# Three token tiles of 88 rows, and a gate product of two columns, in a two-layer decoder trunk

## What is computed

```
logits = (h @ router).astype(jnp.float32)
top_v, top_i = lax.top_k(logits, TOP_K)
gates = jax.nn.softmax(top_v, axis=-1)
combine = jnp.sum(jax.nn.one_hot(top_i, N_EXPERTS) * gates[..., None], axis=-2)
for e in range(N_EXPERTS):
    y = y + combine[..., e:e + 1] * swiglu(h, wg[e], wu[e], wd[e])
```

## Time and profile before

| what | us |
|---|---|
| median of 3 runs | 1030.96 |
| the three runs | 1040.16, 1030.94, 1030.96 |
| span of the profiled execution, first to last instruction | 1036.4 |
| PE busy in it | 961.1 (93%) |
| DVE, ACT, POOL busy | 700.9, 583.8, 193.1 |
| mean granted clock of TensorE | 0.953 |

### The profile page before, as it was taken

One profiled execution on the slowest core, in us unless ns is written; L12 is line 12 of the kernel. 1 busy time (PEld: TensorE's weight loads), 2 busy tenths in 40 slices (PEclk: granted clock), 3 DMA queues, 4 the chain that ended last, 5 costly groups with the idle time before them and its releaser, 6 DMA issues.

```text
span 1036.4 us, 16514 instructions
## 1 busy us (share of the span) xinstructions
PE 961.1 (93%) x5967; PEld 859.6 (83%) x5967; DVE 700.9 (68%) x816; ACT 583.8 (56%) x727; POOL 193.1 (19%) x160
## 2 busy tenths in 40 slices
PE   1798999999999999899979999999999999999998
PEld 0698989999999999798957777787878787878787
DVE  0579747476656547974463356888888888888863
ACT  0565447554445346544442356777777877777742
POOL 0217308421212121730630000010101000000000
PEclk9999879999999999987975899999999999999997
DMA  9374204776699537420342247999898989898921
GB/s 276 86 202 121 82 1 143 199 219 182 182 250 260 159 105 201 122 82 1 113 163 84 86 138 316 389 345 343 330 358 327 364 307 382 301 385 293 376 83 43
DMA packets 171160, 217.62 MB, mean 210 GB/s; under 512 B 6896, under 2 KB 141232, under 8 KB 170974
## 3 DMA queue, kind: packets, MB, share of 16 engines
q1 hardware_dynamic: 163287, 206.25, 59.5%
q10 hardware_dynamic: 6455, 5.54, 1.8%
q0 software_dynamic: 1376, 5.27, 1.6%
HBM read 210.06 MB, written 7.43 MB: 210 GB/s over the span
## 4 chain that ended last, share of the span: by engine, by line
PE 66%; DVE 14%; ACT 8%; issue 6%; POOL 3%; DMA 2%; ACTq 2%; DVEq 0%; SPq 0%; POOLq 0%
PE bank L1599 21%; PE bank L1329 9%; PE bank L1331 8%; PE bank L1330 8%; DVE sb_w_lo L1103 6%; PE bank L1573 4%; ACT sb_w_hi L733 3%; PE bank L1358 2%; PE bank L1469 2%; PE bank L1399 2%; PE bank L1653 2%; ACTq L510 1%; DMA sb_raw<-in_ffn_w_up_dram 1%; DVE at_act_e L1206 1%; POOL at_state L467 1%
## 5 line engine op out<-in xcount | busy, mean ns | idle before, releaser
L890 DVE TENSOR_TENSOR sb_w_lo<-sb_raw,sb_w_hi 128x1024 fp32r<-128x1024 f32 (+1 forms) x116 | 161.8, 1397 | 79.8 <-ACT sb_w_hi L521 77.9
L1329 PE MATMUL bank<-at_act_hi,sb_w_hi 128*128 128x264 f32 x672 | 193.7, 288 | 9.5 <-DVE sb_w_lo L890 6.7
L521 ACT ACTIVATE sb_w_hi<-sb_raw 128x1024 fp32r<-128x1024 f32 (+1 forms) x116 | 126.9, 1101 | 133.9 <-PE bank L1331 114.5
L1103 DVE TENSOR_TENSOR sb_w_lo<-sb_raw,sb_w_hi 128x1408 fp32r<-128x1408 f32 (+1 forms) x104 | 154.4, 1497 | 58.2 <-ACT sb_w_hi L733 58.2
L1331 PE MATMUL bank<-at_act_hi,sb_w_lo 128*128 128x264 f32 x672 | 191.2, 285 | 0.0
L1330 PE MATMUL bank<-at_act_lo,sb_w_hi 128*128 128x264 f32 x672 | 191.1, 284 | 0.0
L1103 DVE TENSOR_TENSOR sb_w_lo<-at_raw_e,sb_w_hi 128x1408 fp32r<-128x1408 f32 (+1 forms) x112 | 158.8, 1450 | 28.3 <-ACT sb_w_hi L733 28.1
L733 ACT ACTIVATE sb_w_hi<-sb_raw 128x1408 fp32r<-128x1408 f32 (+1 forms) x104 | 131.3, 1262 | 73.0 <-PE bank L1599 72.8
L733 ACT ACTIVATE sb_w_hi<-at_raw_e 128x1408 fp32r<-128x1408 f32 (+1 forms) x112 | 138.4, 1243 | 42.2 <-PE bank L1599 38.5
L1329 PEld LDWEIGHTS bank<-at_act_hi,sb_w_hi 128*128 128x128 f32 x672 | 127.7, 190 | 10.2 <-issue 8.3
L1330 PEld LDWEIGHTS bank<-at_act_lo,sb_w_hi 128*128 128x128 f32 x672 | 127.7, 190 | 0.1
(11 more groups left out here) (263 smaller groups left out, 1631.8 us busy)
## 6 DMA issues: line engine op xcount, KB each, us to landing
sb_raw<-in_moe_w_up_dram SPq DMA_DIRECT2D x36, 704.0 KB, 7.2
at_raw_e<-in_moe_w_down_dram SPq DMA_DIRECT2D x49, 512.0 KB, 4.5
at_raw_e<-in_moe_w_gate_dram SPq DMA_DIRECT2D x35, 704.0 KB, 7.8
sb_raw<-in_w_in_dram SPq DMA_DIRECT2D x40, 512.0 KB, 4.0
sb_raw<-in_moe_w_gate_dram SPq DMA_DIRECT2D x29, 704.0 KB, 6.3
sb_raw<-in_moe_w_down_dram SPq DMA_DIRECT2D x39, 512.0 KB, 4.3
at_raw_e<-in_moe_w_up_dram SPq DMA_DIRECT2D x28, 704.0 KB, 6.3
sb_raw<-in_ffn_w_gate_dram SPq DMA_DIRECT2D x22, 512.0 KB, 3.9
```

The lines of the kernel that those rows point to most:

```text
L521: act.activation(w_hi[s][:, 0:kts, :], raw[s][:, 0:kts, :], ACT.Copy).then_inc(hi_done, 1)
L890: dve.tensor_tensor(w_lo[s][:, 0:kts, :], raw[s][:, 0:kts, :], w_hi[s][:, 0:kts, :].bitcast(f32), ALU.subtract).then_inc(lo_done, 1)
L1103: dve.tensor_tensor(lo, raw_e[raw_slot(j, turn)][:, 0:kts_cols, :], hi.bitcast(f32), ALU.subtract).then_inc(moe_lo, 1)
L1329: pe.matmul(out[:, 0:T], w_hi[s][:, k, :], hi[:, c, :], start=(c == 0), stop=False)
```

## The change

The three tiles become 88 rows each. The last one holds the prompt's last 80 tokens and the 8 sample tokens, so its load and its store are two DMAs each. Where DVE did two instructions for the wide tiles and the small one, it does one on 88 rows. For the gate of each slot DVE makes two parts of `gates`, one rounded to fp32r and the rest, next to each other (`gate_parts`), PE takes both as two columns of one product with fp32r operands, and DVE adds the two results with a reduction where it copied before. PE waits for step 24 (`HALVED`) there, where it waited for step 26.

```diff
--- before.py
+++ after.py
@@ -22,7 +22,9 @@
 EPS = 1e-6
 CAP = 128
 SEG = 128
-TOKEN_TILES = ((0, 128), (128, 128), (256, DEC))
+ROWS = T // 3
+TOKEN_TILES = ((0, ROWS), (ROWS, ROWS), (2 * ROWS, ROWS))
+LAST_PROMPT = SEQ - 2 * ROWS
 LEVELS = (1, 2, 4, 8, 16, 32, 64)
 PAD = 16
 
@@ -116,6 +118,7 @@
         rstd_tok = sb("rstd_tok", [128, 3])
         tops = sb("tops", [128, 4, 3])
         gates = sb("gates", [128, 3, N_EXPERTS])
+        gate_parts = sb("gate_parts", [128, 3, N_EXPERTS, 2], f32r)
         slot = sb("slot", [128, 3, N_EXPERTS])
         over = sb("over", [128, 3, N_EXPERTS])
         slot_gate = sb("slot_gate", [128, N_EXPERTS])
@@ -277,7 +280,7 @@
         HG_SUMS = ((5, slice(0, HEADS * SEG), slice(0, SEG)), (6, slice(0, HEADS * DEC), slice(SEQ, T)), (4, slice(0, HEADS * SEG), slice(SEG, SEQ)))
         PIECES = ((0, 512), (512, 512), (1024, 384))
 
-        CHOSEN, GAP, ROUTED = 9, 17, 26
+        CHOSEN, GAP, HALVED, ROUTED = 8, 16, 24, 27
 
         SQUARED = [0] + [KT + n * (2 * KT - 1) for n in range(4)]
         NORM_SUMS = ((3, 0), (4, 0), (4, 1))
@@ -377,12 +380,13 @@
                             sp.dma_start(dst[:, :, :], a[name][0][ds(e, 1), :, ds(f * 128, 128)].rearrange("a (k p) n -> p (a k) n", p=128)).then_inc(all_w, 16)
                         sp.dma_start(down_w_all[:, :], a["moe_w_down"][0][ds(e, 1), ds(f * 128, 128), :].rearrange("a p n -> p (a n)")).then_inc(all_w, 16)
             sp.end_ifs()
-            for i, (_, rows) in enumerate(TOKEN_TILES):
+            for i, (t0, rows) in enumerate(TOKEN_TILES):
                 sp.wait_ge(y_left, i + 1)
                 sp.wait_ge(y_right, i + 1)
-                dst = o["y_prompt"][0, 128 * i:128 * (i + 1), :] if i < 2 else o["y_sample"][:, 0, :]
-                sp.dma_start(dst, y_rows[0:rows, i, :]).then_inc(y_out, 16)
-            sp.wait_ge(y_out, 16 * 3)
+                prompt = min(rows, SEQ - t0)
+                sp.dma_start(o["y_prompt"][0, t0:t0 + prompt, :], y_rows[0:prompt, i, :]).then_inc(y_out, 16)
+            sp.dma_start(o["y_sample"][:, 0, :], y_rows[LAST_PROMPT:ROWS, 2, :]).then_inc(y_out, 16)
+            sp.wait_ge(y_out, 16 * 4)
 
 
         @block.gpsimd
@@ -500,9 +504,10 @@
         @block.scalar
         def _(act):
             for i in range(2):
-                act.dma_start(x_rows[:, i, :], a["x_prompt"][0, 128 * i:128 * (i + 1), :]).then_inc(x_in, 16)
-            act.dma_start(x_rows[0:DEC, 2, :], a["x_sample"][:, 0, :]).then_inc(x_in, 16)
-            act.wait_ge(x_in, 48)
+                act.dma_start(x_rows[0:ROWS, i, :], a["x_prompt"][0, ROWS * i:ROWS * (i + 1), :]).then_inc(x_in, 16)
+            act.dma_start(x_rows[0:LAST_PROMPT, 2, :], a["x_prompt"][0, 2 * ROWS:SEQ, :]).then_inc(x_in, 16)
+            act.dma_start(x_rows[LAST_PROMPT:ROWS, 2, :], a["x_sample"][:, 0, :]).then_inc(x_in, 16)
+            act.wait_ge(x_in, 64)
             act.dma_start(consts[:, C_BEFORE:], a["consts"][:, C_BEFORE:]).then_inc(tables_in, 16)
             act.dma_start(pool_past[:, :], a["state_pool"][0].rearrange("b r c -> (b r) c")).then_inc(past_in, 16)
             act.dma_start(pool_w[:, :, :], a["pool_w"][0].rearrange("g c d -> c g d")).then_inc(pool_w_in, 16)
@@ -744,7 +749,7 @@
             act.dma_start(h_saved, scaled_m[:, :, :].rearrange("p k t -> p (k t)")).then_inc(h_out, 16)
             split_e(1, FE)
 
-            act.wait_ge(rstd_turned, 2)
+            act.wait_ge(rstd_turned, 1)
             for i, (_, rows) in enumerate(TOKEN_TILES):
                 for c in range(2):
                     act.wait_ge(h_turned, 2 * i + c + 1)
@@ -1122,10 +1127,8 @@
             dve.tensor_tensor(logit_rows[:, :], bank[6][0:N_EXPERTS, 0:T], rstd[0:N_EXPERTS, :], ALU.mult).then_inc(logits_scaled, 1)
             dve.wait_ge(logits_zeroed, 1)
             dve.wait_ge(tokens_turned, 1)
-            n_last = TOKEN_TILES[2][1]
-            spread_rstd = bank[5][:, 128:512].rearrange("p (i t) -> p i t", i=3)
-            dve.tensor_copy(rstd_tok[:, 0:2], spread_rstd[:, 0:2, 0]).then_inc(rstd_turned, 1)
-            dve.tensor_copy(rstd_tok[0:n_last, 2:3], spread_rstd[0:n_last, 2, 0:1]).then_inc(rstd_turned, 1)
+            spread_rstd = bank[5][0:ROWS, 128:512].rearrange("p (i t) -> p i t", i=3)
+            dve.tensor_copy(rstd_tok[0:ROWS, :], spread_rstd[:, :, 0]).then_inc(rstd_turned, 1)
             steps = [0]
 
             def step_of(ins, last=True):
@@ -1134,8 +1137,7 @@
                 steps[0] += 1
                 if last:
                     dve.wait_ge(route, steps[0])
-            step_of(dve.tensor_copy(logits[:, 0:2, :], bank[5][:, 0:16].rearrange("p (i e) -> p i e", i=2)), last=False)
-            step_of(dve.tensor_copy(logits[0:n_last, 2, :], bank[5][0:n_last, 16:24]))
+            step_of(dve.tensor_copy(logits[0:ROWS, :, :], bank[5][0:ROWS, 0:24].rearrange("p (i e) -> p i e", i=3)))
 
             wide = [128, 3, N_EXPERTS, N_EXPERTS]
             each = logits[:, :, :].unsqueeze(2).broadcast_to(wide)
@@ -1160,8 +1162,8 @@
                 rest_of_tokens(n)
 
             dve.wait_ge(placed, 1)
-            flat = slot[:, :, :].rearrange("p i e -> p (i e)")
-            step_of(dve.scalar_tensor_tensor(flat, bank[7][:, 0:24], 1.0, chosen[:, :, :].rearrange("p i e -> p (i e)"), ALU.add, ALU.mult))
+            flat = slot[0:ROWS, :, :].rearrange("p i e -> p (i e)")
+            step_of(dve.scalar_tensor_tensor(flat, bank[7][0:ROWS, 0:24], 1.0, chosen[0:ROWS, :, :].rearrange("p i e -> p (i e)"), ALU.add, ALU.mult))
             step_of(dve.tensor_scalar(flat, flat, -1.0, None, ALU.add))
             step_of(dve.tensor_tensor(tops[:, 1, :], tops[:, 1, :], tops[:, 0, :], ALU.subtract), last=False)
             dve.wait_ge(h_out, 16)
@@ -1186,9 +1188,11 @@
             step_of(dve.tensor_tensor(gates[:, :, :], first[:, :, :], tops[:, 2, :].unsqueeze(2).broadcast_to(per), ALU.mult), last=False)
             step_of(dve.tensor_tensor(second[:, :, :], second[:, :, :], tops[:, 3, :].unsqueeze(2).broadcast_to(per), ALU.mult))
             step_of(dve.tensor_tensor(gates[:, :, :], gates[:, :, :], second[:, :, :], ALU.add))
+            step_of(dve.tensor_copy(gate_parts[:, :, :, 0], gates[:, :, :]))
+            step_of(dve.tensor_tensor(gate_parts[:, :, :, 1], gates[:, :, :], gate_parts[:, :, :, 0].bitcast(f32), ALU.subtract), last=False)
             step_of(dve.tensor_reduce(longest[:, :], bank[7][:, 24:32], AX.X, ALU.max))
             step_of(dve.tensor_copy(longest_i[:, :], longest[:, :]), last=False)
-            step_of(dve.scalar_tensor_tensor(over[:, :, :], slot[:, :, :], float(CAP), gates[:, :, :], ALU.is_ge, ALU.mult))
+            step_of(dve.scalar_tensor_tensor(over[0:ROWS, :, :], slot[0:ROWS, :, :], float(CAP), gates[0:ROWS, :, :], ALU.is_ge, ALU.mult))
             assert steps[0] == ROUTED, steps[0]
             dve.wait_ge(unit_used, LAST_UNIT)
             for c in range(2):
@@ -1224,7 +1228,7 @@
                     split_e(j - HEAD_UNITS, FE, turn=0)
                 if j == 3:
                     dve.wait_ge(gate_slots, 1)
-                    dve.tensor_copy(slot_gate[:, :], bank[5][:, 0:N_EXPERTS]).then_inc(y_lo_done, 1)
+                    dve.tensor_reduce(slot_gate[:, :], bank[5][:, 0:2 * N_EXPERTS].rearrange("p (e s) -> p e s", s=2), AX.X, ALU.add).then_inc(y_lo_done, 1)
                 if 0 <= j - 3 < 12:
                     rest_of_packed(4 + j - 3)
 
...
@@ -1551,7 +1555,7 @@
                     pe.wait_ge(route, CHOSEN)
                     for ii, (_, r) in enumerate(TOKEN_TILES):
                         for jj in range(ii):
-                            pe.matmul(bank[7][:, 8 * ii:8 * (ii + 1)], ones, chosen[:, jj, :], start=(jj == 0), stop=False)
+                            pe.matmul(bank[7][:, 8 * ii:8 * (ii + 1)], ones[0:r, :], chosen[0:r, jj, :], start=(jj == 0), stop=False)
                         pe.matmul(bank[7][:, 8 * ii:8 * (ii + 1)], before[0:r, :], chosen[0:r, ii, :], start=(ii == 0), stop=True)
                     for ii, (_, r) in enumerate(TOKEN_TILES):
                         mm = pe.matmul(bank[7][:, 24:32], ones[0:r, :], chosen[0:r, ii, :], start=(ii == 0), stop=(ii == 2))
@@ -1619,10 +1623,10 @@
                 unit_e(("gate", "up")[j // KT], j % KT, j)
                 if j == 0:
                     pe.wait_ge(hot, 6)
-                    pe.wait_ge(route, ROUTED)
+                    pe.wait_ge(route, HALVED)
                     for e in range(N_EXPERTS):
                         for i, (_, rows) in enumerate(TOKEN_TILES):
-                            mm = pe.matmul(bank[5][:, e:e + 1], token_hot[0:rows, i, e, :].bitcast(f32), gates[0:rows, i, e:e + 1], start=(i == 0), stop=(i == 2))
+                            mm = pe.matmul(bank[5][:, 2 * e:2 * e + 2], token_hot[0:rows, i, e, :], gate_parts[0:rows, i, e, :], start=(i == 0), stop=(i == 2))
                     mm.then_inc(gate_slots, 1)
                 if j < N_EXPERTS:
```

(2 more changed lines are left out.)

2 lines of the change are left out of this document (1 added, 1 removed).

## The result

| | kernel before | kernel changed |
|---|---|---|
| median, us | 1033.09 of 4 runs (1030.94 to 1040.16) | 1022.36 of 4 runs (1019.06 to 1023.74) |
| ratio, 95% interval | | 0.9868, 0.9829 to 0.9908 |
| span of the profiled execution, us | 1036.4 | 1020.5 |
| its own time, us | 1038.2, if the same 1.85 lie around the span | 1022.35 |
| mean granted clock | 0.953 | 0.957 |

The span fell by 15.9 us where the sum said 28.3. Every run for which time and span are both on record takes 1.7 to 1.9 us more than its span, so the profiled execution of the kernel before took about 1038.2 us. It was none of the three runs given ahead of the prediction, and 1040.16 was not its own time.

What follows compares the result with a forecast made beforehand. PE was taken to set the pace, with a low clock in part of the run. The terms summed to -28.3 us, a span of 1008; with 2 us taken off the saving, 1030.96 - 26 = 1005 us, range 998 to 1013.

Steps and rivals of the forecast that it cites:

- the sum: All terms of the forecast added, against the profiled execution's span of 1036.4 us: -28.3 us, a span of 1008.
- Term 3: First four gathers, eight runs of six products: no changes of height, clock rising after 5.0 us; -7.1 us.
- The rival on the array's use: Clock stays low through gathers and unit 0, since 88 rows use less of the array than 128; 1009.5 us, chance 0.17.
- Term 1: Start: last 12 transposes of x shorter, -0.7 us; x tiles by four DMAs for three, +0.2; together -0.5.
- Terms 4, 5 and 6: Unit 0 at full clock, -1.6 us; gate products of each slot, -6.0; from there to 577.90 us, -5.0 and +0.9.
- Rival 1: The rival on the array's use: term 3 at -4.7, term 4 at 0, sum -23.5, 1009.5 us; chance 0.17.
- term 6: First hot rows, gather, unit 1, hot rows: full clock, no height change, -5.0 us; +0.9 for a possible clock fall.
- Term 7: From 577.90 us to unit 12: turns of unit, hot rows and gather take 3.67 us for 4.67; -10.0 us.
- Term 8: End: sums of squares by token load 88 columns, last output in two DMAs; +1.2 us, ends -0.3 and +2.9.

Runs made afterwards that it cites:

- e1: The changed kernel with the gathers on 128 rows, rows 88 to 127 being zero; 1013.57 us, ratio 0.9760 to the kernel before.
- e2: The changed kernel with each load and store of 88 rows made by two DMAs, of 80 and 8 rows; 1016.83 us, ratio 0.9790 to the kernel before.
- e12: The changed kernel once more, nothing altered, timed beside the kernel before; 1021.47 us, ratio 0.9848 to the kernel before.

## Why the prediction was wrong, point by point

- **Term 3, the step that failed**: "without gaps they look like the units that raise the clock after 4.2 to 4.4 us". They do not. Units have 128 rows, these gathers 88, and the profiles have a step between 88 and 96 rows: the clock stayed low through all 10.2 us of the gathers, and term 3 gave 4.5 us for 7.1. With the height raised (e1) the rise came 4.2 us after the start; the tenth is luck, since eleven profiles have 3.6 to 4.7. The rival on the array's use had the mechanism as found, and got a chance of 0.17, because the eight busy runs of six that did not raise the clock were read as a matter of gaps. They too had a mean height of 88 rows, (128 + 128 + 8) / 3.
- **Term 1** was wrong in its path. It counted 0.7 us for the transposes of x, which did get shorter (2.02 us for 3.35), but PE then waits for DVE's part of the first weights all the same, and the first unit starts 0.7 us later:

```profile
35.49 0.56 PE L1329 MATMUL bank<-at_act_hi,sb_w_hi 128*128 128x264 f32 x1 [5.58 <-DVE sb_w_lo L890]
...
36.22 0.56 PE L1333 MATMUL bank<-at_act_hi,sb_w_hi 128*128 128x264 f32 x1 [6.48 <-DVE sb_w_lo L895]
```

The first row is the kernel before, the second the changed one. Of the 0.7 us, 0.2 are left at the first logit transpose. Why the weights' part came later is open; splitting the transfers (e2) did not change it.

- **Terms 4, 5 and 6** follow from the step that failed in term 3: unit 0 at 3.65 us, 24 products at 4.98 (4.8 was the low-clock figure), 6.97 us for 4.9. Rival 1 gave -4.7, 0 and -5.2 for terms 3 to 5, and -4.5, 0 and -4.0 were measured. It left term 6 as it was, and there 2.1 us more were lost: the clock rose only behind unit 1.
- **Term 7** was right: turns of 3.62 us for 3.67. So was the reading of the changes of height: 24 products at the low clock are 0.21 apart throughout.
- **Term 8** was mis-sized. Of its 3.5 us, 0.8 are the sums, as the load by columns said (4.62 us for 3.81 from start to next); 2.5 are the stores, for 0.4 forecast. That "the DMA engines have the same bytes" was true and beside the point: fewer engines had them (1.4 us), and more of them came last, to which the other 1.1 are put down without a run. The second half of the sums and of the transposes was at the low clock in both profiles; in e12, where it was not, the whole end took 14.3 us for 17.8.
- **Behind unit 12** 1.0 us came that no term had. In the changed kernel ACT waits 2.98 us there for the first weights of the next expert, and the clock is low for 3.4 us from 614.95. In e12, where the clock did not fall there, the same stretch took 398.22 us, 0.7 over before. What of it is due to the faster turns ahead was not tried.
- **The median**: 1030.96 was the low end of the kernel's spread, some 6 us under the later medians, and so the wrong base for a saving that was read from a span of 1036.4; the 2 us allowed for that were too few. Against 1037.34 the measured gain is 15.9 us, where rival 1's sum had 23.5. So rival 1's 1009.5 was 13 us too low as well: its clock in the gathers was right, and its terms 1, 6 and 8 and its base were not.
